# A third buffer for the experts' gate-up weights, loaded behind the first gather of token rows

## The reference, cut to what matters

```python
x = x + gate1 * mix
h = rms_norm(x, norm2_w) * (1 + scale2) + shift2
pg = softmax(h @ wg)                     # 4 expert groups, the best one is taken
g_sel, pg_sel = argmax(pg), max(pg)
pf = softmax((h @ we)[group g_sel])      # 8 experts in it, the best two are taken
top_p, top_i = top_k(pf, 2)
combine = one_hot(8 * g_sel + top_i) * pg_sel * top_p / sum(top_p)
gate, up = h @ w_gate[e], h @ w_up[e]    # 32 experts, each 1024 x 256, twice
act = silu(gate) * up * combine
x = x + gate2 * sum_e(act @ w_down[e])   # each 256 x 1024
y = rms_norm(x, final_norm_w)
```

## Time and profile before

| | |
|---|---|
| three timed runs | 1565.11, 1566.45, 1566.69 us; median 1566.45 |
| the profiled execution, its own time | 1567.05 us |
| its span | 1565.3 us |
| TensorE matmul busy | 1388.5 us (89%) |
| TensorE weight load | 1003.0 us (64%) |
| VectorE, ScalarE, GpSimd busy | 541.2, 284.2, 129.9 us |
| DMA | 250.85 MB, mean 160 GB/s over the span |
| gate-up weights | 32 loads of 2048 KB, median 18.0 us from issue to landing |
| gathers, scatters | 16 each, median 24.6 and 17.8 us from issue to landing |

### The profile page before, as it was taken

One profiled execution on the slowest core, in us unless ns is written; L12 is line 12 of the kernel. 1 busy time (PEld: TensorE's weight loads), 2 busy tenths in 40 slices (PEclk: granted clock), 3 DMA queues, 4 the chain that ended last, 5 costly groups with the idle time before them and its releaser, 6 DMA issues. The chain is left out here.

```text
span 1565.3 us, 19083 instructions
## 1 busy us (share of the span) xinstructions
PE 1388.5 (89%) x7109; PEld 1003.0 (64%) x7109; DVE 541.2 (35%) x1173; ACT 284.2 (18%) x587; POOL 129.9 (8%) x260
## 2 busy tenths in 40 slices
PE   4999999999999998999788875999999778778873
PEld 2787767888778776777576763788878533222322
DVE  1101377656568654011045536531011411010014
ACT  2201211212224412011121211400000321110111
POOL 0233000000000000232100002000000011111101
PEclk9999999999999999999989876999999879998995
DMA  8553223332331333565430012312235349999954
GB/s 339 146 133 103 82 62 114 121 108 67 108 113 55 108 120 112 172 210 178 144 135 28 27 41 108 110 57 80 68 111 228 135 166 425 424 423 424 410 233 179
DMA packets 62206, 250.85 MB, mean 160 GB/s; under 512 B 10058, under 2 KB 20714, under 8 KB 53002
## 3 DMA queue, kind: packets, MB, share of 16 engines
q1 hardware_dynamic: 42130, 185.31, 32.8%
q10 hardware_dynamic: 10264, 44.97, 8.0%
q0 software_dynamic: 9728, 19.42, 3.7%
HBM read 234.47 MB, written 22.91 MB: 164 GB/s over the span
## 5 line engine op out<-in xcount | busy, mean ns | idle before, releaser
L339 PE MATMUL psum<-arena 128*128 128x272 f32 x3008 | 709.8, 395 | 16.8 <-PEq L1531 10.5
L339 PEld LDWEIGHTS psum<-arena 128*128 128x128 f32 x3008 | 570.5, 191 | 152.6 <-issue 30.4
L2174 PE MATMUL psum<-arena 128*64 128x512 f32 x512 | 129.8, 664 | 36.8 <-issue 18.0
L1094 PE MATMUL psum<-arena 128*128 128x272 f32 x512 | 123.9, 400 | 0.0
L2174 PEld LDWEIGHTS psum<-arena 128*64 128x64 f32 x512 | 42.2, 150 | 114.2 <-issue 94.8
L1094 PEld LDWEIGHTS psum<-arena 128*128 128x128 f32 x512 | 96.9, 192 | 26.0 <-DVE arena L1227 4.1
L1375 PE MATMUL psum<-arena 128*128 128x272 f32 x256 | 65.8, 412 | 0.0
L2256 DVE TENSOR_TENSOR arena<-arena,psum 128x256 f32<-128x256 f32 x16 | 6.8, 422 | 168.8 <-ACT arena L2243 168.8
L930 DVE MATCH_REPLACE8 arena<-arena 32x1056 f32<-32x1056 f32 (+3 forms) x80 | 64.9, 817 | 0.0
L927 DVE MAX8 arena<-arena 32x8 f32<-32x1056 f32 (+3 forms) x80 | 63.4, 825 | 0.9 <-DVE arena L660 0.3
L2195 PE MATMUL psum<-arena 128*64 128x512 f32 x256 | 58.5, 597 | 1.2 <-DVE arena L2264 1.2
(11 more groups left out here) (335 smaller groups left out, 1277.3 us busy)
## 6 DMA issues: line engine op xcount, KB each, us to landing
arena<-in_weights SPq DMA_DIRECT2D x153, 512.0 KB, 3.7
arena<-in_w_gu SPq DMA_DIRECT2D x32, 2048.0 KB, 18.0
arena<-in_w_down ACTq DMA_DIRECT2D x28, 1024.0 KB, 17.4
arena<-in_weights ACTq DMA_DIRECT2D x16, 512.0 KB, 4.3
arena<-in_x SPq DMA_DIRECT2D x2, 2176.0 KB, 11.0
arena<-in_pages_k POOLq DMA_DIRECT2D x32, 128.0 KB, 3.2
arena<-in_pages_k SPq DMA_DIRECT2D x32, 128.0 KB, 2.3
arena<-in_pages_v SPq DMA_DIRECT2D x32, 128.0 KB, 3.3
```

Of the source, the lines that this page charges most:

```text
L339: mm = pe.matmul(out[:, h, :], lhsT=w_of(n, c), rhs=act[:, c, h * HALF:(h + 1) * HALF], start=(c == 0), stop=(c == DC - 1))
L1094: mm = pe.matmul(psum[:, bank, 0:HALF], lhsT=w_of(n, c), rhs=act_of[:, c, h * HALF:(h + 1) * HALF], start=(c == 0), stop=(c == DC - 1))
L2174: mm = pe.matmul(psum[CAP * e:CAP * e + CAP, 2 + k, :].rearrange("p (o f) -> p o f", o=2), lhsT=xgT[:, k, at:at + CAP], rhs=wv[:, c], star ...
```

## The change

The gate-up weights get a third buffer. Its first expert lies in the place of `hT`, its second in 4096 words that end 192 below `a_w` (the end of `merged` and most of `rows11`). Pair p uses buffer p % 3, with a semaphore for each. Pairs 0 and 1 are loaded as before (the two counts on which they wait change places and are both there from the start of the stage). SyncE then waits for the router's result as before and, new, for the landing of gather 0; after it pair 2 is loaded at once, and pair p from 3 on when `gate_up(p - 3)` is done. TensorE waits for the semaphore of buffer p % 3. Nothing else is changed: order of TensorE, GpSimd's queue, down weights.

```diff
@@ -1805,10 +1805,15 @@
-        gath, scat, wgu_full, wdn_full = (s_gath, s_gath1), (s_scat, s_scat1), (s_wgu, s_wgu1), (s_wdn, s_wdn1)
+        gath, scat, wdn_full = (s_gath, s_gath1), (s_scat, s_scat1), (s_wdn, s_wdn1)
+        wgu_full = (s_wgu, s_wgu1, sem("wgu_loaded2"))
+        GU = 3
+        GU_USES = [len(range(k, NP, GU)) for k in range(GU)]
 
         a_w = a_xb + DC * NT + 2 * D
-        w_gu = [A.at(a_q, 2, 2 * DC * FF), A.at(a_ring, 2, 2 * DC * FF)]
+        W_GU = 2 * DC * FF
+        w_gu = [(A.at(a_q, W_GU), A.at(a_q + W_GU, W_GU)), (A.at(a_ring, W_GU), A.at(a_ring + W_GU, W_GU)),
+                (A.at(a_h, W_GU), A.at(a_w - 192 - W_GU, W_GU))]
@@ -1819,7 +1824,7 @@
-        assert a_e + 7680 + 2 * NP <= a_xb + DC * NT
+        assert a_e + 7680 + 2 * NP <= a_w - 192 - W_GU
@@ -2097,9 +2102,10 @@
                 def gate_up_in(r, p):
-                    sp.wait_ge(s_gu, r * NP + (p + 1))
+
+                    sp.wait_ge(s_gu, r * NP + (p if p >= GU else (2, 1, 1)[p]))
                     for e in range(2):
-                        sp.dma_start(w_gu[p % 2][:, e, :], ins["w_gu"][2 * p + e]).then_inc(wgu_full[p % 2], 16)
+                        sp.dma_start(w_gu[p % GU][e], ins["w_gu"][2 * p + e]).then_inc(wgu_full[p % GU], 16)
@@ -2115,6 +2121,7 @@
                     sp.wait_ge(s_slot, 1)
                     sp.reg_load(trips, rounds_i[0:1, 0:1])
+                    sp.wait_ge(gath[0], r * (8 * NP) + 16)
                     for p in range(2, NP):
                         gate_up_in(r, p)
@@ -2165,11 +2172,11 @@
-                    pe.wait_ge(wgu_full[k], r * (16 * NP) + (p // 2 * 32 + 32))
+                    pe.wait_ge(wgu_full[p % GU], r * (32 * GU_USES[p % GU]) + (p // GU * 32 + 32))
                     pe.wait_ge(s_act, r * NP + (p + 1))
                     for c in range(DC):
                         for e in range(2):
-                            wv = w_gu[k][:, e, :].rearrange("p (o c f) -> p c o f", o=2, c=DC)
+                            wv = w_gu[p % GU][e].rearrange("p (o c f) -> p c o f", o=2, c=DC)
```

## The result

The changed kernel took 1559.42 us (median of 5 runs, 1555.44 to 1561.47), the kernel before 1566.69 us in the same series (median of 5). The ratio is 0.9942, with a 95% interval of 0.9925 to 0.9959: 0.6% faster. Forecast were 1559.0 us. A second series, run beside the experiments, gave 1561.31 against 1568.04 us, ratio 0.9957 (0.9943 to 0.9972). The profiled execution took 1559.6 us, its span is 1557.9 us.

What follows compares the result with a forecast made beforehand. The experts' stage was taken as a weight stream at full DMA share with TensorE behind it, the gather loop right behind. Head start 0, middle 0 and end -7.4 us gave 1559.0 us, range 1556.0 to 1564.0.

Steps and rivals of the forecast that it cites:

- The head start: Ahead of the expert stream (1266 to 1279 us, DMA share 0.14): pair 2's load puts 10.0 us of work ahead.
- The middle: Pairs 3 to 13: gain 0, the gather loop keeps 16.74 us a pair and waits move to the transposes.
- the clock: At the last two gate-ups, as a rival: slow clock takes 3.4 us, gain 4.0, 1562.4 us; chance 0.10.
- The turns: In the DMA queues: each gets one packet a turn, so a gather takes 25.1 us against 4.0 in an idle machine.
- slower rival: In the gather loop, also called the slower case: gathers lose turns to the fuller queue, 1575.3 us; chance 0.06.
- The end: Last pairs: SyncE's queue ends one pair sooner, gather 15 lands at 1495.0, three TensorE waits go, -7.4 us.
- The sum: Whole kernel: 0 + 0 - 7.4 us, median from 1566.45 to 1559.0 us; chance 0.60.
- The whole head start: Over the whole stream, a rival: all 10.0 us arrive, the middle giving 2.6 us, 1556.5 us; chance 0.12.
- The renamed wait: At the end, a rival: gather 15 stays near 1500.4, only 2.66 us before gate-up 15 go, 1563.8 us; chance 0.12.

Runs made afterwards that it cites:

- e3: Changed kernel with gather p issued ahead of scatter p - 4 instead of behind it; stage 253.9 and 254.1 us, ratios to kernel before 0.9954 and 0.9945.
- e9: Changed kernel with 3 unused filler matmuls before the gathered rows' transposes of pairs 3 to 14; stage 258.6 us, ratio to kernel before 0.9959.
- e7: Changed kernel with 12 unused filler matmuls before the gathered rows' transposes of pairs 3 to 14; stage 328.0 us, ratio to kernel before 1.0425.
- e5: Changed kernel with all down weights loaded on SyncE's queue instead of ScalarE's; stage 256.5 us, ratio to kernel before 0.9953.
- e8: Kernel before, two buffers and no head start, with the gate-up weights of pair 15 not loaded; stage 258.3 us, ratio 0.9970.
- e2: Changed kernel with only pair 2's first expert loaded early, the second waiting for gate-up 0; stage 263.7 us, ratio to kernel before 1.0006.

## Why the prediction was right

*The head start: 10.0 us.* Right in size and place. The DMA share in the hole rose to 0.98, pair 3 went out when gate-up 0 was done, and with the gather out of the way (e3) the stage of the profiles is 9.2 and 9.0 us shorter than before. Gather 2 beside the load took 11.3 us in the second profile (4.2 before; the prediction took about 10) and cost nothing: gate-up 2 starts at 26.9 us of the stage before and 27.1 after.

*The middle: 0.* Right in the main, for the reason given: 32.0 us of waits for weights became 27.9 us more of waits for gathers, and the pace was 16.3 us a pair (gate-up 10 to 14) where 16.7 was forecast. Not right in detail: gate-up 4 was to start 1.5 us sooner and started 1.2 us later in the stage (58.4 against 57.2), behind a wait of 4.96 us for its gather and transposes and down of 1.97 and 5.08 us. And gather 15 is issued 2.8 us later than before (211.5 against 208.7). Idle time now stands ahead of transposes and down, and 8 of the downs ran slowly; but e9, with 4 slow ones, issued gather 15 no sooner, so what delays it stays open. The prediction had priced the clock for the last gate-ups and called it hidden in the middle; the last gate-ups stayed at 7.09 us.

*The turns.* The prediction read them from equal packet counts, and its slower rival leant on the same counts. They don't show it: each pair needs 256 rows from every queue (two experts of 128 for either kind of weights, 128 places gathered and 128 scattered), so the counts come out equal in whatever order the packets go. In e7, where TensorE was the bound and the queues took only 0.85 of the engines' time, they were as equal (packets, MB, share, 1320 to 1480 us):

```profile
q1 hardware_dynamic: 2261, 32.88, 50.8%
q10 hardware_dynamic: 2224, 16.12, 27.4%
q0 software_dynamic: 2285, 4.47, 7.2%
```

What bears the turns out is e5.

*The end: -7.4 us.* Right in mechanism (e8), 1.1 us too large. Transposes 14 waited for their gather and began 0.7 us later in the stage than before, so the 2.94 us wait before gate-up 14 gave 2.3; and transposes 15 still waited 0.63 us where the prediction had none. The mis-sized term is the landing of the last gathers. Gather 15 was forecast for 228.5 us of the stage (1495.0) and came at 230.4 (1495.5 in this profile, whose stage began 1.4 us sooner). SyncE's queue kept its forecast: the last gate-up load landed at 1490.02 us, 224.9 of the stage, where 225.0 was forecast (1491.5). DMA of the changed kernel by queue (packets, MB and share), 1486 to 1490 us:

```profile
q10 hardware_dynamic: 59, 0.45, 41.0%
q0 software_dynamic: 29, 0.08, 4.9%
q1 hardware_dynamic: 5, 0.05, 2.9%
```

The engines were half idle, and still the gather was not in. The times of its 16 counts say why: 15 of them had come by 1490.38 us, sooner than the forecast, and the last came at 1495.51. In the second profile 14 had come by 1490.50 and the last two at 1492.53 and 1497.12. The prediction had scaled the length of a mean turn, and the landing goes by the last part. What put that part behind, no run tested.

*The sum.* The stage gave 6.3 and 6.9 us in two profiles, and the medians 7.3 and 6.7. That the first median lies 0.4 us from the forecast is luck within the scatter of the runs; that the gain is 6 to 7 us and not 10 is what the argument said.

*The rivals.* The whole head start needs the gather out of the way (e3, in the stage of the profiles; the time of the whole kernel doesn't show it). The renamed wait is what half a head start gives (e2); with half the bytes ahead, the change would have been worth nothing. The slower case stays out: in the middle scatters took 16.4 us instead of 17.9 and gathers, in the second profile, 23.6 instead of 25.1, so the fuller queue took nothing from GpSimd's.

## What to carry to other kernels

Where DMA is at full share and the compute engine waits behind it, as here, look for the idle DMA time that a further buffer can fill ahead of the stream: three buffers without the early load gave nothing. Whether that time comes out at the other end depends on the next queue in line: here gate-up weights, gathered rows and down weights all wanted the same number of packets, so each cure moved the wait to the next, and half a head start was lost whole. Count packets by queue, not only bytes: here small transfers beside large ones took the longer the more queues there were. But equal counts say nothing of how queues share where each round of work needs the same number from all of them; change the number of queues and look at the times. And the end of a transfer is the end of its last part: ask when that comes, not when the mean does.

## What the runs showed of the hardware that was not expected

Putting down weights and gate-up weights into one queue made GpSimd's scatters 1.6 times as fast (16.4 to 10.3 us) at the same bytes and the same 1.01 share.

The 16 counts of one gather come far apart. Gather 15 of the kernel before was issued at 1475.20 us; 12 counts had come by 1487.62, the others came at 1491.80, 1495.61, 1498.74 and 1500.45.

Where idle time stands decides what runs slowly behind it. Before, it stood ahead of gate-up (8.78 us instead of 7.09); after, ahead of the transposes, and a wait of 4.62 us was followed by 1.97 us of transposes (1.09 without) and 5.77 us of down (3.65), that is up to 1.8 times as long, where the clock's two levels, 1.2 and 2.4 GHz, are a factor of 2 apart. Gate-up behind them was at 7.09 us in every pair from 1 on. Not every wait had this price: gate-up 14 before took 7.09 us behind 2.94 us of idle time.

A 32-bit matmul of 512 columns for one expert alone took 0.87 us (10.46 us for 12, which show as 24 records). Gate-up of a pair is 8 x 2 = 16 such matmuls by the kernel's loops, shown as 32 records, and not 32 as written ahead of the prediction (down is 8, not 16). They alternate between two experts, whose results lie in different halves of the PSUM rows, and took 7.09 us, 0.44 each: half of 0.87, as if two ran side by side. No run tested that reading.
